# Moving 24 modulation columns from the first feed-forward stage of a four-layer transformer kernel into its second mixer

## What is computed

```
for l in range(DEPTH):                                 # first_block; second_block has the same frame
    ada = cs @ ada_w[l] + ada_b[l]                     # cs = silu(c), ada has 6 * 1024 values
    sh1, sc1, g1, sh2, sc2, g2 = split(ada)
    h = rmsnorm(x) * (1 + sc1) + sh1
    x = x + g1 * token_mixer(h, ...)
    h = rmsnorm(x) * (1 + sc2) + sh2
    f = swiglu(h, ...) if l % 2 == 0 else moe_swiglu(h, ...)
    x = x + g2 * f
```

## Time and profile before

| | |
|---|---|
| median of 3 runs | 2861.55 us (2857.86 to 2862.45) |
| the profiled execution: its own time | 2865.6 us |
| its span, first to last instruction | 2863.9 us |
| outside the span | 1.7 us |
| TensorE matmuls busy | 2793.9 us (98%) |
| TensorE weight loads busy | 2137.5 us (75%) |
| VectorE busy | 945.7 us (33%) |
| ScalarE busy | 530.1 us (19%) |
| mean granted TensorE clock | 0.987 of full speed |
| read from HBM | 702.65 MB, 246 GB/s over the span |

### The profile page before, as it was taken

How to read it: one execution, slowest core, us unless ns; L and a number is a source line. 1 busy time by engine, 2 the same in 40 slices (tenths; PEclk the granted TensorE clock), 3 DMA queues, 4 the chain that set the end, 5 groups by cost and what they waited for, 6 DMA issues and landing times.

```text
span 2863.9 us, 42555 instructions
## 1 busy us (share of the span) xinstructions
PE 2793.9 (98%) x17857; PEld 2137.5 (75%) x17857; DVE 945.7 (33%) x2191; ACT 530.1 (19%) x1104; POOL 94.1 (3%) x181
## 2 busy tenths in 40 slices
PE   7999999899999999999999999999999998999999
PEld 6789988778888655445536537778998896889888
DVE  2654443354411011101101104554355226643330
ACT  3332000233210001001101103243121023331110
POOL 0000111000000000000000000000011000000000
PEclk9999999999989999999999999999999999999999
DMA  8535786533289979998998994332377542323432
GB/s 367 196 127 222 298 305 259 207 118 125 96 339 426 425 299 426 425 415 352 425 428 344 425 409 165 116 118 100 140 254 257 220 171 111 118 107 141 179 118 96
DMA packets 71468, 706.44 MB, mean 247 GB/s; under 512 B 7920, under 2 KB 8176, under 8 KB 31728
## 3 DMA queue, kind: packets, MB, share of 16 engines
q1 hardware_dynamic: 45792, 610.92, 52.7%
q0 software_dynamic: 25488, 92.81, 9.0%
HBM read 702.65 MB, written 1.05 MB: 246 GB/s over the span
## 4 chain that ended last, share of the span: by engine, by line
PE 67%; DMA 2%; DVE 2%; ACT 1%; issue 0%; DVEq 0%; ACTq 0%; SPq 0%
PE psum L969 28%; PE psum L1210 7%; PE psum L1222 6%; PE psum L1270 5%; PE psum L1267 4%; PE psum L984 4%; PE psum L1193 4%; PE psum L1273 2%; DMA ring<-in_m 2%; PE psum L1168 1%; PE psum L1033 1%; PE psum L1231 1%; PE psum L1285 1%; PE psum L1119 1%; PE psum L993 1%; PE psum L1083 1%
## 5 line engine op out<-in xcount | busy, mean ns | idle before, releaser
L969 PE MATMUL psum<-hT,ring 128*128 128x256 f32 x4544 | 994.6, 380 | 0.0
L969 PEld LDWEIGHTS psum<-hT,ring 128*128 128x128 f32 x4544 | 859.9, 190 | 122.2 <-ACT work L1526 3.3
L969 PE MATMUL psum<-work,ring 128*128 128x256 f32 x1624 | 353.4, 379 | 0.0
L969 PEld LDWEIGHTS psum<-work,ring 128*128 128x128 f32 x1624 | 308.1, 190 | 42.5 <-ACT work L1395 0.7
L2197 DVE CUSTOM_DVE_ANT_0 mod_in<-mod_in,c_rows,cols 128x1024 f32<-128x1024 f32 x128 | 161.0, 1279 | 64.5 <-DMA mod_in<-in_mods 64.4
L1210 PE MATMUL psum<-ring,work 128*32 128x256 f32 x2688 | 179.2, 380 | 1.4 <-DVE work L2161 0.7
L984 PE MATMUL psum<-hT,ring 128*128 128x128 f32 x1408 | 163.3, 277 | 2.3 <-ACT hT L1471 1.2
L2161 DVE TENSOR_TENSOR work<-work,psum 128x128 f32<-128x128 f32 x119 | 34.2, 287 | 395.0 <-ACT work L1565 387.5
L984 PEld LDWEIGHTS psum<-hT,ring 128*128 128x128 f32 x1408 | 161.5, 194 | 2.9 <-DVE hT L1825 1.3
L1222 PE MATMUL psum<-ring,work 128*64 128x256 f32 x1216 | 139.6, 382 | 0.0
L2318 POOL DMA_DIRECT2D mod_in<-in_mods x152 | 80.7, 531 | 1776.2 <-DVE ada L2197 1685.8
(11 more groups left out here) (248 smaller groups left out, 2585.9 us busy)
## 6 DMA issues: line engine op xcount, KB each, us to landing
ring<-in_m SPq DMA_DIRECT2D x76, 2048.0 KB, 17.6
ring<-in_w_in SPq DMA_DIRECT2D x46, 2048.0 KB, 7.9
mod_in<-in_mods POOLq DMA_DIRECT2D x176, 512.0 KB, 6.0
ring<-in_m SPq DMA_DIRECT2D x42, 1792.0 KB, 17.4
work<-in_m SPq DMA_DIRECT2D x36, 2048.0 KB, 17.9
ring<-in_up SPq DMA_DIRECT2D x22, 2048.0 KB, 7.7
work<-in_m SPq DMA_DIRECT2D x22, 1792.0 KB, 17.4
ring<-in_f SPq DMA_DIRECT2D x11, 2048.0 KB, 8.8
```

The source lines that it names most:

```text
L969: last = mm(gbank(it["bank"])[:, j, :], wt[:, k, col0 + j * P:col0 + (j + 1) * P], rhs[:, k0 + k, :], start=(n == 0), stop=(n == total - 1))
```

## The change

The 24 early columns of the third layer (`layer` 2) leave the first FFN: 12 that were spread over its up units, 2 behind the first down unit and 10 behind the second. Four of layer 1's eight columns behind the first down unit move behind the second. In the second mixer these 24 follow layer 1's last 12, and all 36 are spread over slots 2 to 29: two columns in slots 2, 5, 9, 12, 16, 19, 23 and 26, one in each other slot. The code below line 417 moves by four lines, so that line 2197 is line 2201 after the change.

```diff
@@ -414,8 +414,12 @@
         slots[19] += [ph("n_sum", nm=n_z), ph("n_fin", nm=n_z)]
-        rest = adas(0, 16, 40) if l == 0 else adas(1, 36, 48)
-        at = (3, 4, 4, 5, 6, 6, 7, 8, 10, 12, 14, 16) + tuple(range(18, 30)) if l == 0 else tuple(range(18, 30))
+        if l == 0:
+            rest = adas(0, 16, 40)
+            at = (3, 4, 4, 5, 6, 6, 7, 8, 10, 12, 14, 16) + tuple(range(18, 30))
+        else:
+            rest = adas(1, 36, 48) + adas(2, 0, EARLY_MODS)
+            at = [2 + 28 * j // len(rest) for j in range(len(rest))]
         for j, it in zip(at, rest):
             slots[j].append(it)
@@ -426,9 +430,9 @@
-            plan.extend(spread(items, adas(0, 40, 48) + adas(1, 0, 28) + adas(2, 0, 12)))
+            plan.extend(spread(items, adas(0, 40, 48) + adas(1, 0, 28)))
             downs = down_units("f2", (), 22, "hid", lambda i: evac("resid", l, 40, 2 * i), last, True)
-            slots = {0: adas(1, 28, 36) + adas(2, 12, 14), 1: adas(2, 14, EARLY_MODS)}
+            slots = {0: adas(1, 28, 32), 1: adas(1, 32, 36)}
             mid = leave("a1m", downs[:3], downs[3:], 6, slots, 2, 1, "a1_mix_g", 0, "a")
```

## The result

The changed kernel takes 2842.99 us (median of 5 runs, 2841.69 to 2848.29). The kernel before, run beside it, takes 2859.20 us (5 runs, 2857.86 to 2862.45). The ratio is 0.9945 (95% interval 0.9930 to 0.9959): 16.2 us or 0.55% faster. Forecast were 2845.5 us and a gain of 16.1 us.

What follows compares the result with a forecast made beforehand. TensorE sets the pace, except at a pause in the first FFN where column loads delay VectorE's third drain. Terms -16.10 + 0 + 0 + 0 = -16.1 us, from the median 2861.55, give 2845.5 us; range 2841 to 2852.

Steps and rivals of the forecast that it cites:

- The main term: First FFN's down part: the wait before the sums of squares goes, with the slower sums; -16.10 us.
- the twin stage: Third layer's FFN, four columns behind each of its first two down units; stretch of 12.51 us against 28.61.
- The warning that the median might gain only 12 us: Profiled execution lay 4 us above the median; part may be the first FFN's wait, then the median gains 12 us.
- The zeros: First FFN's up part and second mixer's slots 2 to 7, 8 to 17 and 18 to 29: 0 us each.
- Up part: First FFN's up units lose twelve of 48 columns, for which TensorE never waited: 0 us.
- Slots 3 to 18: Second mixer's stretch still lasts 141.51 us with columns in it, as the first mixer's does: 0 us.
- The pair of slot 9: Second mixer's scan: two columns (2.56 us) fit into 3.08 us of VectorE's idle time, 0.5 us left.
- The drain of unit 24: Second mixer's pa and pb units: drain some 2 us late, 0.9 us left; 0 us, bound 3.5 us.
- What is late next: First FFN: fourth column behind the second down unit, done by 491.9, 2.7 us before the third unit is complete.
- Landings of 9.7 or 12.4 us all through the drains: Second mixer's drains: late loads give back 8.6 us (2854.1 us, chance 0.09) or 14.9 us (2860.4 us, 0.04).
- The low clock moving into full work: First FFN, 500 to 525 us: lower clock granted as long without the pause costs 6.8 us, 2852.3 us; chance 0.06.
- The slower case: Second mixer's drains: landings of 22.5 us, the trace's longest, cost 38.5 us, 2884.0 us; chance 0.03.

Runs made afterwards that it cites:

- e1: Changed kernel with the up part's twelve early columns put back there, only the down part's twelve moved; 2844.12 us, ratio 0.9948.
- e7: Changed kernel with the old arrangement in the third layer's FFN, 22 columns in its up part, 10 + 10 in its down part; 2858.94 us (one run).
- e2: Changed kernel with 10 + 10 columns in the first FFN's down part again, only its up part lighter by twelve; 2860.68 us, ratio 1.0004.
- e10: Kernel before, all columns still in the first FFN, but twelve ahead of the first down unit's drain and 4 + 4 behind; 2843.31 us, ratio 0.9942.
- e4: Kernel before with 10 + 7 columns in the first FFN's down part, three moved to the second mixer; 2854.37 us (one run).
- e12: Kernel before with the two 2 MB ring loads issued as the third down unit ends cut to 256 KB each; 2853.63 us (one run).
- e8: Changed kernel with all 36 second-mixer columns in slots 18 to 29, three a slot; 2877.41 us (one run).
- e9: Changed kernel with 24 second-mixer columns in slots 8 to 15, three a slot, and 12 in slots 18 to 29; 2843.95 us (one run).
- e11: Kernel before with the ten columns behind the second down unit loading half their weights, 256 KB in place of 512 KB; 2854.80 us (one run).

## Why the prediction held

**The main term** was -16.10 us, taken from the twin stage, and -16.11 us was measured at that place; the medians moved by 16.2. Its two parts, idle time and slower sums, both went. The sums take 2.68 us from start to start, as the twin's. e1 and e7 show it from both sides: the gain comes with the down part alone, and ten columns in the twin take 12.5 us away. That the two numbers agree to 0.01 us is luck: the loss they are measured against was 16.1 us in one trace and 13.3 in another with as many columns there (e2), 12.5 in the twin (e7). That about 16 us is typical is shown by the medians alone, 16.2 us here, 16.1 in e1 and 15.5 in e10. The warning that the median might gain only 12 us didn't come true. The forecast time itself lay 2.5 us high, mostly because the median before fell from 2861.55 (3 runs) to 2859.20 (5 runs).

**The zeros** held. Up part: e2, ratio 1.0004. Slots 3 to 18: 141.52 us for a forecast of 141.51. The pair of slot 9 was to leave 0.5 us and left 0.66. The drain of unit 24 was forecast for 733.1 us (less the 19.57 us of the shift 713.5) and came at 713.67, without a wait on TensorE. Its bound of 3.5 us didn't come into play: the loads of the drains landed in 3.7/5.2/9.7 us.

**What is late next** was forecast with 2.7 us to spare for the fourth column. It was done at 484.2, 7.0 us ahead of 491.12, because its load, issued at 474.69, took 8.0 us and not 12.4.

**What the prediction had incomplete** is the cause of the pause: "With three buffers, and a refill only after the column that used the buffer, twenty columns in two bursts are more than the loads deliver." It leaves out why the loads are late. The runs show that the ring's two 2 MB loads, which SyncE issues as the third unit ends, make the last column loads land in 9.9 to 13.1 us (before, e4) and not 5 (e12), and that this alone is about half of the pause or more; the same meeting stands behind the two units before. What three buffers cost without it is open. The number wasn't hurt, since it came from a comparison of two stages that both have these ring loads, and not from a model of the loads. Where the times of single columns were used, for e4, the forecast was off by more: an expected 8.7 us against 6.69.

**The rivals.** Landings of 9.7 or 12.4 us all through the drains: they weren't there, median 5.2. The low clock moving into full work: from 500 to 525 us it is 1.00. The slower case: the place and mechanism are real, shown by e8 at three columns a slot, 13.6 us above the kernel before on its chip (2877.41 against 2863.84, one run each); with one and two a slot the drains catch up. The port rule of the Trainium skill ("SBUF — State Buffer", "SBUF: two separate sides") didn't show: GpSimd's issues take 530 ns through the whole scan, and 527 to 530 ns in e9 with VectorE busy for 19.8 of 20 us. The page states the lock-out of descriptor writes for VectorE's two-port performance modes, which a float32 `tensor_copy` triggers; a column multiplies two inputs out of SBUF, so the rule may not bear on it at all.

**Still open**: how the rest of the pause divides between the count of buffers and the earlier pairs of ring loads, and whether a shared rate or the order of completion makes the column loads late. More than three buffers wasn't tried. No version that computes everything is clearly below the changed kernel; e1 and e10 equal it within their intervals.

## What to carry over

Optional work in the queue of an in-order engine is not priced by its duration but by the latest of its inputs: ten 1.28 us operations cost nothing by themselves and 16 us through their loads. Put such work where a late finish meets slack (ahead of an early drain, as in e10, or into slots that the critical engine fills, as in e9), and not just before the drain that the next stage waits for; look there also for large transfers that start at the same time. And if the program has the same stage elsewhere with another setting, the difference of the two stretches in one trace is a better price than a sum of parts.

## Of the hardware, not expected

- In the down part, a 512 KB load that lands in 3.6 to 5.8 us without large neighbours takes 8 to 14 us when two 2 MB loads of another queue are issued up to 5 us ahead of it or 1 us behind it (column load at 493.97, ring loads at 494.77: 9.9 us). The changed kernel has the short end of this, 8.0 to 8.1 us for three loads 2.4 to 4.8 us behind the pair of 472.3. Halving the load helps less than shortening its neighbours: 7.2 to 10.8 us (e11) against 4.7 to 5.4 (e12), one run each.
- After the pause, the 24 sums take 4.2 to 5.3 us from start to start and not 2.7, and the longer pauses, from 5.8 to 14.1 us in six traces, don't have the slower sums.
- Two executions of nearly the same program differ by 3.5 us within the first 60 us, with a different granted clock (0.73 against 0.86 from 25 to 50 us), though the change touches nothing there, so one pair of traces gave 23.9 us for a change worth 16.2.
